# Decoder layers with a mixture of experts: the last overflow block's rows are added by products with a matrix of token places, and the odd experts' sum is read while the overflow blocks run

## The reference

```python
scores = sigmoid(t @ w_router)                       # 512 tokens, 64 experts
_, eidx = top_k(scores + router_bias, 8)
g = take_along_axis(scores, eidx); g = g / g.sum() * 2.5
...
# tokens sorted by expert, in blocks of 128; per block:
out = (silu(xb @ w1[e]) * (xb @ w3[e])) @ w2[e] * gs[:, None]
routed = segment_sum(out, row_tok, num_segments=512)
x = x + gate2 * (routed + shared)                    # gate2: per column, from c
```

## Time and profile before

| | |
|---|---|
| median of 3 runs | 2369.04 us (2365.8 to 2372.58) |
| profiled execution | 2366.73 us, span 2364.9 us |
| TensorE busy | 2258.3 us, 95% of the span |
| VectorE / ScalarE / GpSimd busy | 65% / 51% / 12% |
| granted TensorE clock, mean | 0.987 of full speed |
| memory | 408.67 MB read, 43.65 MB written |

### The profile page before, as it was taken

The page is one execution under the profiler, slowest core; times in us unless marked ns, Lnnn a source line. Parts: engine busy times, 40 slices in busy tenths (PEclk is TensorE's granted clock), DMA queues, the critical chain, the costliest instruction groups (busy, mean ns, idle before and its releaser), DMA issues.

```text
span 2364.9 us, 30566 instructions
## 1 busy us (share of the span) xinstructions
PE 2258.3 (95%) x10242; PEld 1760.4 (74%) x10242; DVE 1538.0 (65%) x2360; ACT 1199.5 (51%) x1774; POOL 292.5 (12%) x248
## 2 busy tenths in 40 slices
PE   7998999899999999997999999999999789999997
PEld 5776566778888888874766788888788457888885
DVE  7789766899999999986654643333442766333344
ACT  4432434588888888874434332333222763322333
POOL 0000000343334334433000000000110000000000
PEclk9999999999999999999999999999999999999999
DMA  8511245799999999995210132233232001322232
GB/s 331 178 54 63 81 169 185 269 360 395 387 393 388 391 391 392 391 328 164 91 52 28 58 116 97 95 106 99 89 98 97 11 30 60 116 98 96 99 107 81
DMA packets 107472, 415.71 MB, mean 176 GB/s; under 512 B 20161, under 2 KB 32705, under 8 KB 82640
## 3 DMA queue, kind: packets, MB, share of 16 engines
q1 hardware_dynamic: 87408, 378.47, 42.7%
q0 software_dynamic: 19504, 34.73, 5.9%
q10 hardware_dynamic: 432, 0.87, 0.1%
HBM read 408.67 MB, written 43.65 MB: 191 GB/s over the span
## 4 chain that ended last, share of the span: by engine, by line
PE 77%; DVE 8%; ACT 5%; issue 5%; DVEq 2%; DMA 1%; POOLq 0%; SPq 0%; POOL 0%; ACTq 0%
PE PS L298 22%; PE PS L300 22%; PE PS L299 21%; ACT wh L192 3%; PE PS L714 3%; PE PS L2010 2%; PE PS L736 2%; DVE wl L197 1%; PE PS L725 1%; DMA ada_wa<-wada 1%; PE PS L2035 1%; DVEq L1285 1%; DVE M L1282 1%; PE PS L1245 1%; DVE HG L2075 0%
## 5 line engine op out<-in xcount | busy, mean ns | idle before, releaser
L197 DVE TENSOR_TENSOR wl<-raw,wh 128x1024 fp32r<-128x1024 f32 x239 | 292.5, 1225 | 357.2 <-ACT wh L192 351.0
L298 PE MATMUL PS<-HTh,wh 128*128 128x512 f32 x1248 | 498.6, 400 | 6.5 <-ACT V L881 2.2
L300 PE MATMUL PS<-HTh,wl 128*128 128x512 f32 x1248 | 486.9, 390 | 0.0
L299 PE MATMUL PS<-HTl,wh 128*128 128x512 f32 x1248 | 486.6, 390 | 0.0
L197 DVE TENSOR_TENSOR wl<-eraw,wh 128x1024 fp32r<-128x1024 f32 x384 | 457.5, 1219 | 16.7 <-ACT wh L192 13.5
L192 ACT ACTIVATE wh<-raw 128x1024 fp32r<-128x1024 f32 x239 | 252.0, 1056 | 362.7 <-PE PS L300 338.7
L192 ACT ACTIVATE wh<-eraw 128x1024 fp32r<-128x1024 f32 x384 | 392.6, 1054 | 17.4 <-PE PS L300 15.0
L298 PEld LDWEIGHTS PS<-HTh,wh 128*128 128x128 f32 x1248 | 234.4, 188 | 72.6 <-issue 13.4
L300 PEld LDWEIGHTS PS<-HTh,wl 128*128 128x128 f32 x1248 | 234.5, 188 | 49.9
L299 PEld LDWEIGHTS PS<-HTl,wh 128*128 128x128 f32 x1248 | 234.7, 188 | 49.7 <-issue 3.4
L298 PE MATMUL PS<-wh,XTh 128*128 128x512 f32 x536 | 221.1, 412 | 1.9 <-DVE wl L2195 1.4
(11 more groups left out here) (413 smaller groups left out, 3454.2 us busy)
## 6 DMA issues: line engine op xcount, KB each, us to landing
eraw<-wstream SPq DMA_DIRECT2D x192, 1024.0 KB
raw<-wstream SPq DMA_DIRECT2D x240, 512.0 KB, 3.3
ada_w<-wada SPq DMA_DIRECT2D x20, 512.0 KB, 5.7
eraw<-wexp SPq DMA_DIRECT2D x9, 1024.0 KB
ada_wb<-wada SPq DMA_DIRECT2D x2, 2048.0 KB, 15.6
ada_l<-wada SPq DMA_DIRECT2D x8, 512.0 KB, 3.4
ada_g<-wada SPq DMA_DIRECT2D x2, 2048.0 KB, 10.3
expert_sum<-LM SPq DMA_DIRECT2D x8, 512.0 KB, 5.4
```

The lines of the kernel that those rows point to most:

```text
L197: nc.vector.tensor_tensor(wl[:, ci % RING, :], src, wh[:, ci % RING, :].bitcast(F32), ALU.subtract).then_inc(split_done, 1)
L298: nc.tensor.matmul(o, lh, rh, start=start, stop=False)
L299: nc.tensor.matmul(o, lh, rl, start=False, stop=False)
L300: return nc.tensor.matmul(o, ll, rh, start=False, stop=stop)
```

## The change

What it does, part by part:

- GpSimd's block casts its token list to float32 as TOK, a column of GS set to 4103 (no token) at the start; scatter, waits and release of YS happen only if another block follows. So the last block's rows stay in PSUM. `last_tokens` is raised when the nest is left, and `rows_whole` asks only for the even sum and the scatters that were made.
- SP reads a row of 0 to 511 in all partitions (TOKENS) and the odd sum (YO, four quarters) as soon as the odd experts have been scattered, in places that the overflow blocks don't use. The even sum (YE, four quarters) is read after `rows_whole`.
- VectorE makes LAST_T, 128 rows by 512 tokens: 1 where the row's token is the column's. ScalarE and VectorE split the last block's rows from PSUM into LAST_H and LAST_L.
- `quarter_turn` makes, per tile, two products with LAST_T and then, into the same bank, four float32 products of YO's sum with the identity in place of four transposes.
- TensorE runs `keep_clock(3)`, waits for the split, then quarter 0. The third split of `mla_in`'s weights on VectorE moves behind the first two tiles.

```diff
@@ places
-            YF = place("YF", [P, 2, 4, NB, 256], 3072)
+            YO = [place(f"YO{q}", [P, NB, 256], at) for q, at in enumerate((2176, 3200, 5376, 7424))]
+            TOKENS = nc.alloc_sbuf_tensor_at("TOKENS", [P, S], F32, offset=HT_AT + 4 * 6 * S)
+            LAST_H = place("LAST_H", [P, D], 18432, F32R)
+            LAST_L = place("LAST_L", [P, D], 19456, F32R)
+            LAST_T = place("LAST_T", [P, S], 20480, F32R)
+            YE = nc.alloc_sbuf_tensor_at("YE", [P, 4, NB, 256], F32, offset=HT_AT + 4 * DT * S)
@@ SP
+                sp.wait_ge(chunk_used, EXPERT1 + RING)
+                sp.wait_ge(gate_at, E)
+                sp.dma_start(TOKENS[:], consts[:, CONST_N:CONST_N + S]).then_inc(sem("tokens_in"), 16)
+                sp.wait_ge(y_out[1], 16 * E // 2)
+                for q in range(4):
+                    sp.dma_start(YO[q][:], ysum[1].rearrange("(b p) (q d) -> q p b d", p=P, q=4)[q]).then_inc(ya_in[q], 16)
                 sp.wait_ge(sem("rows_whole"), 1)
-                sp.wait_ge(sem("ya_free"), 1)
                 for q in range(4):
-                    for s in range(2):
-                        sp.dma_start(YF[:, s, q, :, :], ysum[s].rearrange("(b p) (q d) -> q p b d", p=P, q=4)[q]
-                                     ).then_inc(ya_in[q], 16)
+                    sp.dma_start(YE[:, q, :, :], ysum[0].rearrange("(b p) (q d) -> q p b d", p=P, q=4)[q]).then_inc(ya_in[q], 16)
@@ GpSimd, block_
                     pool.drain()
+                    pool.tensor_copy(TOK, YIXC[:, y:y + 1])
                     with pool.If(more[pool.engine] > i * GROUP + (p + 1)):
                         more_gate(p + 1, i)
                         more_gather(pool, p + 2, code_of(p + 2, i), i)
-                    pool.wait_ge(ov["y"], i * GROUP + (p + 2))
-                    pool.sem_inc(passed_pool, 1)
-                    pool.indirect_dma_start(out=ysum[0], out_offset=bass.IndirectOffsetOnAxis(ap=YIXC[:, y:y + 1], axis=0),
...
-                    with pool.If(more[pool.engine] > i * GROUP + (p + 1)):
+                        pool.wait_ge(ov["y"], i * GROUP + (p + 2))
+                        pool.sem_inc(passed_pool, 1)
+                        pool.indirect_dma_start(out=ysum[0],
...
                         pool.wait_ge(ov["rows"], i * (16 * GROUP) + 16 * (p + 3))
                         pool.sem_inc(passed_pool, 1)
-                    pool.wait_ge(ov["out"], i * (16 * GROUP) + 16 * (p + 1))
-                    pool.sem_inc(ov["sent"], 1)
+                        pool.wait_ge(ov["out"], i * (16 * GROUP) + 16 * (p + 1))
+                        pool.sem_inc(ov["sent"], 1)
...
-                for s in range(2):
-                    pool.wait_ge(y_out[s], 16 * E // 2)
+                pool.drain()
+                pool.sem_inc(sem("last_tokens"), 1)
+                pool.wait_ge(y_out[0], 16 * E // 2)
                 pool.sem_inc(sem("rows_whole"), 1)
@@ ScalarE: YS only under If(count > p + 1), then
+                act.wait_ge(sem("last_out"), 1)
+                nc.scalar.activation(LAST_H[:], PS[:, 6:8, :].rearrange("p a b -> p (a b)"), ACT.Copy).then_inc(sem("last_high"), 1)
@@ VectorE
-                dve.drain().then_inc(sem("ya_free"), 1)
-                for c in range(AHEAD):
+                dve.wait_ge(sem("tokens_in"), 16)
+                dve.wait_ge(sem("last_tokens"), 1)
+                nc.vector.tensor_scalar(LAST_T[:], TOKENS[:], TOK, None, ALU.is_equal).then_inc(sem("last_out"), 1)
+                dve.wait_ge(sem("last_high"), 1)
+                nc.vector.tensor_tensor(LAST_L[:], PS[:, 6:8, :].rearrange("p a b -> p (a b)"), LAST_H[:].bitcast(F32),
+                                        ALU.subtract).then_inc(sem("last_out"), 1)
+                for c in range(2):
                     split_dve(dve, EXPERT1 + c)
@@ TensorE, quarter_turn
+                    r = slice(m * P, (m + 1) * P)
+                    nc.tensor.matmul(PS[:, SUM_BANK[m % 4], :], LAST_H[:, r], LAST_T[:], start=True, stop=False)
+                    nc.tensor.matmul(PS[:, SUM_BANK[m % 4], :], LAST_L[:, r], LAST_T[:], start=False, stop=False)
                     for tb in range(NB):
-                        mm = nc.tensor.transpose(PS[:, SUM_BANK[m % 4], tb * P:(tb + 1) * P],
-                                                 YF[:, 0, q, tb, m % 2 * P:(m % 2 + 1) * P], const("ident"))
+                        mm = nc.tensor.matmul(PS[:, SUM_BANK[m % 4], tb * P:(tb + 1) * P],
+                                              YO[q][:, tb, m % 2 * P:(m % 2 + 1) * P], const("ident"), start=False,
+                                              stop=tb == NB - 1)
@@ VectorE and TensorE behind it
-                nc.vector.tensor_tensor(YF[:, 0, 0, :, :], YF[:, 0, 0, :, :], YF[:, 1, 0, :, :], ALU.add).then_inc(sem("ya_first"), 1)
+                nc.vector.tensor_tensor(YO[0][:], YO[0][:], YE[:, 0, :, :], ALU.add).then_inc(sem("ya_first"), 1)
                 for m in range(DT):
...
+                    if m == 1:
+                        split_dve(dve, EXPERT1 + 2)
...
-                pe.wait_ge(sem("rows_whole"), 1)
-                keep_clock(6)
+                keep_clock(3)
+                pe.wait_ge(sem("last_out"), 2)
```

More of the change, by code:

```diff
@@ L1552, in build @@
             YIXC = place("YIXC", [P, 4], 11016, I32)
-            GS = place("GS", [P, 6], 11024)
+            GS = place("GS", [P, 8], 11024)
+            TOK = GS[:, 7:8]
             TB = place("TB", [1, 3 * 68], 11032, I32)
@@ L1770, in _ @@
                 nc.vector.memset(LM[:], 0.0).then_inc(sem("lm_zero"), 1)
+                nc.vector.memset(TOK, EMPTY)
                 nc.vector.tensor_copy(LS[:], LC[:, 384:448])
```

21 lines of the change are left out of this document (13 added, 8 removed).

## The result

| | before | changed |
|---|---|---|
| median | 2368.48 us (22 runs, 2365.29 to 2372.58) | 2373.3 us (22 runs, 2365.76 to 2383.43) |
| ratio | | 1.0022, 95% interval 1.0014 to 1.0031 |
| profiled execution, span | 2366.73, 2364.9 us | 2370.54, 2368.7 us |

The changed kernel is slower by 0.22%, inside the 0.3% that I had named as no difference. The spread says more: 17.7 us between its fastest and slowest run against 7.3 before. So a small loss is there, 4.8 us between the medians where the forecast had 2 to 2.5, and part of it is a tail of long runs.

A forecast was written before the change was run, and what follows sets the result against it. TensorE, busy 95% of the span, was taken to bound the kernel; -6.5 (earlier start) +6.5 (added work) +2.5 (clock) gave +2.5 on the 2369.0 median, written as 2371 us, range 2362 to 2379.

The forecast's parts named there:

- The forecast case: Whole kernel: the time lands within a few us of 2371; chance 0.70.
- its band: Whole kernel: about 2365 to 2376 us for the forecast alone, from the terms' ends and the runs' spread.
- the sum's terms: Routed experts to second block: -6.5 earlier start, +6.5 added TensorE work, +2.5 clock, giving +2.5 us.
- what goes and what takes its place: Overflow blocks to quarter 0: last scatter goes, rows_whole at 1096.5, VectorE's chain gates quarter 0 at 1103.9, 6.5 earlier.
- signs of being wrong: TensorE waiting in overflow blocks, quarters under 2.5 us at full clock, or rows_whole before 1095 or after 1099.
- contention of the early reads: Overflow blocks, path to rows_whole: early reads delay indirect transfers by 0.5 us, bounds nothing and 5.4.
- The rule set beside it: Block 2's gather: DMA engines alternate between queues packet by packet, so its lone part takes twice as long, sum 1.0 higher.
- Rival (b): Block 2's gather: early reads collide with it, 5.4 instead of 0.5 plus some 2, giving 2378; chance 0.12.
- the products: Quarter turns on TensorE: float32 products at 0.133 per instruction, 1.52 per tile, 3.04 per quarter against 0.9; stage +6.5 us.
- the clock, 2.5: Quarter 0 on TensorE: some 6 us at half clock after idling lose 2.5 us, ends nothing and 3.4.
- GpSimd's sums would stop slowing VectorE: mla_in stage: GpSimd's three sums done by about 1111, before quarter 2, which earns nothing as TensorE bounds.
- LAST_H was put at 1.03: ScalarE's split after LAST_T: 1.03 us like YS, from 1097.2 to 1098.3.

The follow-up runs named there:

- e12: The changed kernel once more, unedited, profiled again: 2374.3 us, ratio 1.0029 to the kernel before.
- e1: Changed kernel with SP holding token numbers and odd sum's reads until block 0's scatter has landed: 2371.57 us, ratio 1.001 to before.
- e4: Changed kernel with the odd sum read late, after rows_whole, as before the change: 2365.45 us, ratio 0.9989 to before.
- e10: The kernel of e4 once more, beside fresh runs of before: 2369.47 us, ratio 1.0003.
- e3: Changed kernel with nine clock-keeping products instead of three ahead of quarter 0: 2367.46 us, ratio 1.0005 to before.
- e2: Changed kernel with identity products made transposes again and LAST's two products cut into 128 tokens each: 2370.09 us, ratio 1.001 to before.
- e11: Changed kernel with three clock-keeping products in front of block 2's transposes: 2372.48 us, ratio 1.0015 to before.
- e5: Changed kernel with GpSimd's first sum waiting for VectorE's addition: 2371.89 us, ratio 1.0012 to before.
- e7: Changed kernel with LAST's products of tiles 0 to 3 made ahead of quarter 0, then three clock-keeping products: 2369.21 us, ratio 1.001 to before.
- e9: Changed kernel with the edits of e1, e5 and e7 together: 2368.45 us, ratio 0.9997 to before.

## Why the prediction was right or wrong

The forecast was 2371.0 us, a change of +2.5; measured were 2373.3, +4.8 between the medians, and up to LAT +1.2 in one profile and +3.0 in the other (e12). The forecast case held, and the slower end of its band is where the time lies, but the sum's terms don't reach it: what carries the median on to +4.8 is in none of them.

- **Right: what goes and what takes its place.** No scatter after block 1's, a way out of 2.5, VectorE's chain and not the read gating quarter 0, no gaps from quarter 0 until the first pair ends. One of its own signs of being wrong came all the same: TensorE waited 2.10 us for a gather in the overflow blocks.
- **Mis-sized: contention of the early reads, 0.5.** I took a gather that ran beside weights and argued that indirect transfers are paced by something other than bandwidth. TensorE took the gather up 6.7 us after its issue instead of 4.5, block 0's scatter landed after 9.0 instead of 6.3, and block 2's copy came 2.6 late; I had given that copy 1.1 (0.5, and two casts of 0.3). Without the early reads `rows_whole` came 2.5 (e1), 3.4 (e4) and 1.7 (e10) sooner. The step that failed is the choice of the row: the weights beside that gather were issued one by one as rings came free, and the odd sum is a burst: the engines' share was 1.0 and more in every two microseconds from 1072 to 1082. The rule set beside it (the Trainium skill, "DMA: Bandwidth & Descriptors", Arbitration) asked for 1.0 more; the trace goes in its direction and beyond its size. Rival (b) named place and sign rightly and overpriced it: about 2.5, not the 5.1 from which it would have decided. With the last copy and cast (3.3 us to `rows_whole`, forecast 3.0) that is the whole of 1098.27 against 1096.5.
- **Mis-sized, other way: the products.** Eight float32 instructions take 0.9 us (0.11 each), as the transposes of the earlier trace rows, and not 8 x 0.133; a tile is 1.35 and a quarter 2.7 instead of 3.04, over four quarters 1.4 us less. The row I took, L736, has products of another place in it.
- **Right in size, within its bounds: the clock, 2.5.** In the first profile the clock returned after 3.1 us of quarter 0 and not 6, and the term is 1.4 (against e3). In e12, the same kernel, it returned after 6.1, and the term is 2.8. Before, the clock fell at about 1097.8, 5.3 us after TensorE's last product, and was back at 1108.0; in both profiles of the changed kernel it fell at about 1101.3, 2.2 to 2.5 us after the last clock-keeping product, and was back at 1108.1 in one and 1111.5 in the other. Why the same program gets one or the other is open.
- **Mis-sized, small:** LAST_T 0.49, not 0.7.
- **The sum by its steps.** Quarter 0 started 5.4 earlier (forecast 6.5), and from there to the last product it is 25.1 us instead of 18.5 (the prediction has 18.6 where its own rows give 18.5): 6.6 with the clock, forecast 9.0. Together +1.2. In e12 it is a start 5.0 earlier and 8.0 more to LAT, +3.0. A forecast start 1.1 to 1.5 too early and a forecast of the work 1.0 to 2.4 too long stand against each other, and the median holds a cost that the sum hasn't: that the total came near is in good part luck.
- **Missed: two engines at one time.** I wrote that GpSimd's sums would stop slowing VectorE, from the earlier trace rows (two splits in 4.24), and did not ask what they would do to the chain in front. In the kernel before, VectorE's splits were done long before the sums' data arrived. The change moved the two next to each other, with 0.8 us between. In a profile where VectorE comes second, the price is 2.0 us (e1), 4.0 (e2) or 6.3 (e11). At equal clock, e5, which differs from the changed kernel by the hold alone, is 2.9 us better, so this is the larger part of the loss. It rests on one set of 11 runs. What the remaining 2.0 are made of, and how much of them is the clock behind the gather's wait (block 2 ended 2.7 us late in e5's profile), stays open.
- **Missed: ScalarE's way out.** LAST_H was put at 1.03 behind LAST_T. It holds in the changed kernel's profile, where GpSimd is later still, and in those of e10 and e12. In the nine other profiles with the new chain (e1 to e5, e7 to e9, e11) LAST_H began 0.7 to 4.2 us after LAST_T was done: there ScalarE's 2.8 to 4.5 us from block 2's end is what VectorE waits for.
- **Missed: what runs by itself.** Behind LAT the same instructions take 1232.5 to 1240.4 us in fourteen profiles, by how long the clock is at 0.50 there: between LAT and the last stretch, from about 2355 on, not at all in e11 (the 1232.5), 14 us in before's, 24 in the changed kernel's (which has 0.5 around 1925, before's has not) and 27 in e12 (the 1240.4). Before's 1236.3 is at the short end of that range, and the 2.6 by which the two profiles differ behind LAT lies well inside it. Whether the change itself moves these stretches can't be told from one profile of the kernel before.

## What to carry to other kernels

Moving a transfer "to where it is hidden" is only free if nothing latency-bound runs there: an indirect gather without slack is such a thing, and a burst of 2 MB beside it cost at least what the read saved. When a chain is shortened, look at which work of other engines its end now meets, and with what margin; here margins of 0.1 to 0.8 us went with a tail of long runs (e3 and e7), even where the median was near before's. And repeat the best variant before believing it: two medians of twelve runs of one kernel were 4 us apart here, and the runs' granted clocks showed that the better one was no gain.

## What the runs showed of the hardware

- A VectorE operation with two inputs in SBUF took 3.1 to 3.4 us instead of 1.22 when GpSimd's own TENSOR_TENSOR had begun before it (e1, e2, e11), and two one-column operations (lamc) 2.36 and 2.37 instead of 0.22 (e11, e2); X's update, whose one tensor input is in PSUM and one in SBUF, took 0.75 beside the same sums. The first of e11's splits ended 1.08 us after GpSimd's first 2.35 us were over. The other way round it is GpSimd that pays: its first sum took 2.63, 3.00, 3.17 and 3.36 us when VectorE's addition had begun 0.81, 0.45, 0.29 and 0.08 us before it (changed, e12, e3, e7), so that it ended 3.45 us after the addition's start each time. By the Trainium skill ("SBUF — State Buffer", Who interferes with whom, and its Summary: rules for kernel authors), a VectorE instruction with two SBUF inputs contends with a GpSimd instruction that reads SBUF, and the second to issue blocks fully; the durations here agree, and a sum of both durations is what a plan should use.
- At full clock a float32 product of 128 columns was two instructions 0.11 us apart, and a transpose one, with the same spacing (0.10 in e2): a factor of two.
- A TensorE wait of 1.1 to 2.1 us in the middle of dense work was followed by 3.4 to 7 us at the lower clock level (0.50) in four of seven cases: e2, e3, e5 and e7, and not the changed kernel, e12 and e9, whose wait of 1.61 was for block 3's gather.
- Leaving the nest of `If`s: from the end of GpSimd's last cast to LAST_T it was 2.8 to 3.5 us, and from the end of block 2's last product to ScalarE's next instruction, where nothing else held it, 2.8 to 4.5 us.
